# Seven products for the down-projection of a SwiGLU block, with its results added to the residual in DRAM

## The reference

```
x = x + gate2 * SwiGLU(RMSNorm(x) * (1 + scale2) + shift2)
swiglu(h) = (silu(h @ w_gate) * (h @ w_up)) @ w_down      # D_FF = 2816 = 22 tiles of 128
```

## Time and profile before

| | us |
|---|---|
| median of three runs | 940.18 |
| the profiled execution | 943.49 |
| its span, first to last instruction | 941.6 |
| TensorE (PE) busy | 919.5 (98%) |
| VectorE busy | 596.2 (63%) |
| ScalarE busy | 405.5 (43%) |
| mean busy share of the DMA engines in the seven-product stages | 0.72 to 0.75 |

### The profile page before, as it was taken

How to read it: one execution, slowest core, us unless ns; L and a number is a source line. 1 busy time by engine, 2 the same in 40 slices (tenths; PEclk the granted TensorE clock), 3 DMA queues, 4 the chain that set the end, 5 groups by cost and what they waited for, 6 DMA issues and landing times.

```text
span 941.6 us, 15995 instructions
## 1 busy us (share of the span) xinstructions
PE 919.5 (98%) x6385; PEld 861.3 (91%) x6385; DVE 596.2 (63%) x1115; ACT 405.5 (43%) x809; POOL 80.5 (9%) x103
## 2 busy tenths in 40 slices
PE   5999999999999999999999999999999999999998
PEld 5689888778887899999999999999999999999998
DVE  3557898899688752332447966743577763367752
ACT  4564344666767722222246644421344431244430
POOL 0000000000000000000000122101233200133100
PEclk7799999999999999999999999999999999999999
DMA  9854343442444123422203278543687843377631
GB/s 370 321 180 157 134 149 120 154 144 68 136 146 152 63 68 90 180 68 90 68 23 109 72 179 166 158 124 79 154 169 177 184 145 112 79 168 188 169 111 70
DMA packets 45546, 129.35 MB, mean 137 GB/s; under 512 B 5216, under 2 KB 10464, under 8 KB 44320
## 3 DMA queue, kind: packets, MB, share of 16 engines
q1 hardware_dynamic: 32288, 102.64, 32.4%
q0 software_dynamic: 12464, 24.91, 14.8%
q10 hardware_dynamic: 720, 0.77, 0.2%
HBM read 114.02 MB, written 4.33 MB: 126 GB/s over the span
## 4 chain that ended last, share of the span: by engine, by line
PE 80%; DMA 7%; DVE 7%; issue 2%; ACT 2%; SPq 1%; DVEq 0%; POOLq 0%; ACTq 0%
PE ps L1589 38%; PE ps L1946 15%; PE ps L1685 13%; DMA stage<-stage 5%; PE ps L1893 4%; PE ps L1811 3%; PE ps L1785 2%; PE ps L1796 2%; PE ps L1638 1%; DVE w_lo L1462 1%; PE ps L1709 1%; DMA x<-w_ada 1%; DVE scr L1499 1%; DVE scr L1107 1%; DMA vec<-vecs 1%
## 5 line engine op out<-in xcount | busy, mean ns | idle before, releaser
L1070 DVE TENSOR_TENSOR w_lo<-stage,w_hi 128x1024 fp32r<-128x1024 f32 x56 | 68.3, 1222 | 77.4 <-ACT w_hi L640 77.2
L1589 PE MATMUL ps<-y_hi,w_hi 128*128 128x320 f32 x480 | 109.6, 309 | 1.6 <-DVE w_lo L1506 1.6
L1589 PE MATMUL ps<-y_hi,w_lo 128*128 128x320 f32 x480 | 109.4, 309 | 0.0
L1589 PE MATMUL ps<-y_lo,w_hi 128*128 128x320 f32 x480 | 109.3, 309 | 0.0
L985 ACT ACTIVATE w_hi<-stage 128x512 fp32r<-128x512 f32 x114 | 67.9, 624 | 89.3 <-DMA stage<-stage 47.7
L640 ACT ACTIVATE w_hi<-stage 128x1024 fp32r<-128x1024 f32 x56 | 59.1, 1061 | 91.4 <-PE ps L1589 50.9
L1462 DVE TENSOR_TENSOR w_lo<-stage,w_hi 128x512 fp32r<-128x512 f32 x114 | 76.3, 685 | 30.6 <-ACT w_hi L985 30.6
L1946 PE MATMUL ps<-m_hi,w_hi 128*128 128x320 f32 x304 | 93.9, 309 | 0.0
L1946 PE MATMUL ps<-m_lo,w_hi 128*128 128x320 f32 x304 | 93.9, 309 | 0.0
L1946 PE MATMUL ps<-m_hi,w_lo 128*128 128x320 f32 x304 | 93.9, 309 | 0.0
L1589 PEld LDWEIGHTS ps<-y_hi,w_hi 128*128 128x128 f32 x480 | 80.2, 188 | 2.1 <-DVE w_lo L1506 2.1
(11 more groups left out here) (210 smaller groups left out, 1995.4 us busy)
## 6 DMA issues: line engine op xcount, KB each, us to landing
stage<-w_main SPq DMA_DIRECT2D x118, 512.0 KB, 3.7
x<-w_ada SPq DMA_DIRECT2D x23, 512.0 KB, 4.6
scr<-w_main POOLq DMA_DIRECT2D x38, 256.0 KB, 4.6
stage<-stage POOLq DMA_DIRECT2D x38, 256.0 KB, 3.3
qk<-w_ada SPq DMA_DIRECT2D x7, 1024.0 KB, 11.7
stage<-w_main POOLq DMA_DIRECT2D x19, 256.0 KB, 5.0
bb<-rpb SPq DMA_DIRECT2D x16, 256.0 KB, 4.2
qk<-w_ada SPq DMA_DIRECT2D x5, 512.0 KB, 3.7
```

What stands on the lines that cost most here:

```text
L1070: dve.tensor_tensor(w_lo[:, slot, :], stage[:, slot, :], w_hi[:, slot, :].bitcast(F32), ALU.subtract).then_inc(lo_done, 1)
L1589: ins = pe.matmul(out[:, half, :], wt[:, w_slot, w], rt[:, rk, half * TH:(half + 1) * TH], start=start and n == 0, stop=stop and n == 2)
```

## The change

- The down-projection is done by seven products too: two output tiles by two halves of the part's hidden tiles by two halves of the tokens. All work from the fourth hidden tile on is one list of 31 jobs (`JOBS`): 5 gate/up jobs and 4 down jobs, 8 and 4, 6 and 4. A down job has 7 x 4 x 3 matmuls in the first two parts and 7 x 3 x 3 in the last (`job_half`: blocks of 384 columns in place of 512). For every job POOL makes the sums of weights.
- The blocks of the hidden tiles (T1 to T4 of activations) are made per part on DVE and split (`y_sums`, `y_sums_high`, `y_sums_low`).
- The residual isn't held in SBUF any more. POOL copies `x` to `y_t` in one transfer (2.6 MB) when it is complete, and each down result, multiplied by gate2 on ACT (`scaled`), is added to `y_t` by a POOL transfer of 320 KB with accumulate: 24 in all (`add_result`). The eight writes of `x` by SP and the 24 `add_gated` on DVE go away.
- The products come in the order A11, S1, A12, S4, S2, S3, A22 (A11, A12, S2, S1, S3, S4, A22 before), so the gate tile's first half and second half are complete after the third and the fifth product. A22 has two places among the split weights.

The order of POOL's instructions and of ACT's and DVE's loops is new:

```diff
-            for g in range(sum(FF_PARTS) - N_STD):
...
+            pool.wait_ge(x1_done, 8)
+            pool.dma_start(y_t.rearrange("p k t -> p (k t)"), x[:, :]).then_inc(x_out, 16)
+            def add_result(j, second):
+                d, n = down_number(j), JOBS[j][2] + second
+                i = d % 2 * 2 + second
+                pool.wait_ge(r_done, 2 * d + second + 1)
...
+                pool.dma_start(y_t[:, n, :], kept[i], accum_op=ALU.add).then_inc(r_out[i], 16)
...
+            for j in range(len(JOBS)):
+                more = j + 1 < len(JOBS)
+                if j and JOBS[j - 1][1] is None:
+                    add_result(j - 1, 1)
+                if more:
+                    s1_s3_first(j + 1)
+                    s2_s3(j + 1)
+                    s4(j + 1)
+                if JOBS[j][1] is None:
+                    add_result(j, 0)
+            add_result(len(JOBS) - 1, 1)
```

`JOBS[j][1]` is the hidden tile of a gate/up job and None for a down job. On ACT:

```diff
+            def scaled(j, second):
...
+                act.wait_ge(c21_done if second else c12_done, j + 1)
...
+                for kind, t in ((0, slice(0, CTX)), (1, slice(CTX, T))):
+                    ins = act.activation(kept[i][:, t], (low_sb if second else high_sb)[:, t], ACT.Identity,
+                                         scale=mod[:, g + kind:g + kind + 1])
+                ins.then_inc(r_done, 1)
...
+            for j in range(len(JOBS)):
+                f, more = JOBS[j][1], j + 1 < len(JOBS)
+                ended = JOBS[j - 1][1] if j else N_STD - 1
+                if ended is not None:
+                    y_high(ended)
+                else:
+                    scaled(j - 1, 1)
+                if more:
+                    left_high("A11", j + 1)
+                copy_p1(j)
+                if ended is not None:
+                    y_sums_high(ended)
+                if more:
+                    left_high("S1", j + 1)
+                    left_high("A22", j + 1)
+                    left_high("A12", j + 1)
+                if f is not None:
+                    half_tanh(j, 0)
+                if more:
+                    left_high("S2", j + 1)
+                if f is not None:
+                    half_tanh(j, 1)
+                else:
+                    scaled(j, 0)
+                if more:
+                    left_high("S4", j + 1)
+                    left_high("S3", j + 1)
+            scaled(len(JOBS) - 1, 1)
```

On DVE and PE:

```diff
+            for j in range(len(JOBS)):
...
+                if j:
+                    c21(j - 1)
+                if ended is not None:
+                    times_up(j - 1) if j else gated_up(ended)
+                left_low("S4", j)
+                left_low("S3", j)
+                if ended is not None:
+                    y_low(ended)
+                    y_sums(ended)
+                if more:
+                    left_low("A11", j + 1)
+                if ended is not None:
+                    y_sums_low(ended)
+                c11(j)
+                if more:
+                    left_low("S1", j + 1)
+                    left_low("A22", j + 1)
+                    left_low("A12", j + 1)
+                u2_v_c12(j)
+                if more:
+                    left_low("S2", j + 1)
+                c22_u3(j)
+                if f is not None:
+                    gate_times(j)
...
+            for j in range(len(JOBS)):
...
+                    free = dict(A11=(p1_copied, j), S1=(v_done, j), A12=(c11_done, j), S4=(c12_done, j),
+                                S2=(v_done, j), S3=(c22_done, j), A22=(c21_done, j))
+                for op in LEFT:
+                    pe.wait_ge(*free[op])
+                    product(op, j)
```

More of the change, by code:

```diff
@@ L590, in _ @@
                 load_unit(u, u % RING)
[L591 to L593 removed]
             sp.wait_ge(out_kv, 64)
[L595 removed]
+            sp.wait_ge(x_out, 16)
+            for i in range(4):
+                sp.wait_ge(r_out[i], 16 * 2 * len(FF_PARTS))
         @block.gpsimd
@@ L981, in left_high @@
                 else:
[L982 to L990, removed]
+                    act.wait_ge({"S1": s1_sum, "S2": s2_sum, "S3": s3_sum, "S4": s4_sum}[op], 16 * (j + 1))
@@ new lines, in left_high, with copy_p1 @@
+                act.wait_ge(*slot_free(op, j))
+                slot, at = left_place(op, j)
+                act.activation(w_hi[:, slot, at:at + job_half(j) * P], left_stage(op, j), ACT.Copy).then_inc(left_hi[op], 1)
+            def copy_p1(j):
+                act.wait_ge(left_used["A11"], j + 1)
+                if j and JOBS[j - 1][1] is not None:
+                    act.wait_ge(a32_done, JOBS[j - 1][1] + 1)
+                elif j:
+                    act.wait_ge(r_done, 2 * down_number(j))
@@ L1018, in _ @@
             t_high(1)
-            a_high(0)
+            y_high(0)
             gate_tanh(1)
@@ L1497, in products_gated, with gate_times, times_up @@
+            def gate_times(j):
+                dve.wait_ge(tanh_done, JOBS[j][1] + 1)
+                own.mark(dve.scalar_tensor_tensor(out=ft_sb, in0=ft_sb, scalar=1.0, in1=high_sb, op0=ALU.add, op1=ALU.mult))
+            def times_up(j):
+                part, f, _ = JOBS[j]
+                i, half = tile_of(f)
                 own.wait()
-                dve.wait_ge(c12_done, g + 1)
-                dve.scalar_tensor_tensor(out=fp[f % 2], in0=up_sb, scalar=0.5, in1=ft[f % 2],
+                dve.wait_ge(c21_done, j + 1)
+                if part and i < half:
+                    dve.wait_ge(r_out[i], 16 * 2 * part)
+                dve.scalar_tensor_tensor(out=product_of(f), in0=low_sb, scalar=0.5, in1=ft_sb,
@@ L1514, in _ @@
             t_sums(1)
-            a_low(0)
+            y_low(0)
             t_low(0)
             t_low(1)
+            y_sums(0)
             gated(1)
@@ L1523, in _ @@
             t_low(3)
-            a_low(1)
+            y_sums_low(0)
+            y_low(1)
+            y_sums(1)
             left_low("S1", 0)
@@ new lines, in right_made, with product @@
+            def right_made(op, j, k):
+                first, half = FF_FIRST[JOBS[j][0]], job_half(j)
+                f = first + k + (half if op in ("A12", "S4") else 0)
+                if op in ("A11", "A12", "S4"):
+                    return a_ready, f + 1
+                return {"S1": y1_lo, "S2": y23_lo_done, "S3": y23_lo_done, "A22": y4_lo}[op], pair_of(f) + 1
+            def product(op, j):
+                pe.wait_ge(left_lo[op], j + 1)
+                if j == 0 and op not in ("A11", "A12", "S4"):
+                    pe.wait_ge(t_ready, ("S1", "S2", "S3", "A22").index(op) + 1)
+                slot, at = left_place(op, j)
+                half = job_half(j)
+                for k in range(half):
+                    if JOBS[j][1] is None and JOBS[j - 1][1] is not None:
+                        pe.wait_ge(*right_made(op, j, k))
```

446 lines of the change are left out of this document (205 added, 241 removed).

## The result

The changed kernel takes 1012.29 us (median of four runs, 1010.64 to 1017.25) against 940.2: ratio 1.077, 95% interval 1.073 to 1.081. It is 72 us slower; 21 were forecast. The profiled execution took 1017.25 us.

What follows compares the result with a forecast made beforehand. The prediction took the kernel before as bound by its number of matmuls on PE, with transfer circles deciding afterwards. Matmuls and idle -21.0, circles +39.4, end +2.2 made +20.6 us on 940.2, so 961 us; 8-in-10 range 944 to 990.

Steps and rivals of the forecast that it cites:

- Matmuls: Down-projection on PE: 924 matmuls in place of 1056, 132 fewer at 0.147 us, -19.4 us; -21.0 with idle time.
- The circle in a down job: Add ahead of S1 on POOL's queue, S1 landing 5.0 plus 0.4: rounds 16.3 us against PE's 12.3; +39.4 us together.
- T: The time at which S4 of job j has landed; the forecast counts its rounds from there.
- The circle in a gate/up job: S4 landing to next S4 landing: 12.5 us, 11.2 in a part's first half; S2 3.3, S4 3.5; nothing lost.
- the thin cover of DVE: Gate/up jobs of second halves: DVE about 12 us against PE's 12.3; taken as 0, up to 5 us at the upper end.
- The lead: End of a part's gate/up jobs: S4 lands 2.2 us ahead of its latest time, 1.5 in the last part's step.
- `scaled` behind T: Down jobs, ACT: `scaled(j-1, 1)` stands behind splits of S4 and S3; otherwise a round would miss by some 0.3 us.
- The end: Last matmul to end of span: C21, `scaled`, POOL and an accumulate's landing, 6.0 us for 3.8, +2.2.
- long transfers: Rival: adds hold the queue twice as long, 1.8 us more in ten rounds, 979; longest landings 988; chance 0.17.
- clock: Rival: PE's clock falls in the waits, four products behind a wait at half pace, 991 us; chance 0.09.
- short landings: Rival: S1 lands after 3.6 + 0.4 and S4 after 3.2, 1.7 less in ten rounds, 944 us; chance 0.13.
- the adds cost nothing: Rival: down rounds stay under 12.3 us, so only the matmuls count, 921.4 us, faster; chance 0.11.

Runs made afterwards that it cites:

- the version with small adds: Against the changed kernel: S1 issued early with adds behind, S3 split before S4, adds cut to 8 of 640 columns (output incomplete); ratio 0.998 to the kernel before.
- the version with plain writes: Against the changed kernel: S1 issued early with adds behind, S3 split before S4, the 24 adds without accumulation (output incomplete); ratio 1.009 to the kernel before.
- The small adds: Against the changed kernel, its queue order kept: every add to `y_t` moves 8 of its 640 columns (output incomplete); ratio 1.044 to the kernel before.
- the better one: Against the changed kernel: S1 of job j+2 issued right behind S4 of job j+1, adds behind it, S3 split before S4; ratio 1.032 with whole adds.
- the filler: Against the changed kernel: 20 small matmuls into an unused bank in each of ten jobs, ahead of products S1 and S4; ratio 1.076 to the kernel before.
- joined adds: Against the changed kernel: S1 early, S3 split first, one 640 KB add per job, last part's units loaded without padding; ratio 1.023 to the kernel before.

## Why the prediction was wrong

The direction, the down jobs as the place and the path of the circle were right. The landing times of the transfers were wrong, in both kinds of job, and they have one thing in common: they were taken from rows in which other transfers stood around them. The measured loss is over three times the forecast. From the issue of S4 of job 1 (552.89) to that of job 30 (996.41) 443.5 us pass. The matmuls of the 29 jobs between need 26 x 12.3 + 3 x 9.2 = 347.4. So 96 us are lost there, where 39.4 were forecast.

- **Matmuls: right.** PE's busy time in the version with small adds is 899.2 us at a clock of 0.995, the "900 us or a little less" of the forecast.
- **The circle in a down job: right in its path, its largest term mis-sized.** Ten rounds took 182.6 us, where 8 x 16.3 + 2 x 14.8 = 160.0 were forecast: 22.6 us of the excess. From T to the issue of S1 it is 3.0 us where 3.3 were forecast, from S2 to S4 3.9 for 3.7. The step that failed is "I take the median 5.0 ... the very place that the add takes, plus 0.4". S1 landed after 7.1 to 9.4 us in the eight rounds of the first two parts and after 6.1 and 5.7 in the last part, 7.4 in the mean of the ten: 2.1 more a round, 21 of the 22.6 us. The place on the queue was the same, the neighbours weren't: an accumulate to DRAM costs more than its bytes (no add landed under 4.5 us, where in the version with plain writes the shortest took 2.4), and the copy for S3, once held back by a wait, follows 0.55 us behind. The small adds confirm the first: with them, S1 lands after 4.8 us in the mean and the round is 15.8. What the copy behind S1 adds wasn't tried by itself.
- **The circle in a gate/up job: wrong.** "Here nothing is lost" failed by its terms "S2's transfer 3.3" and "S4's transfer 3.5". The forecast left out that the split which frees the copy's place now stands behind T, so that the copy and the completion of S3 are issued close ahead of S2 and S4. S4 landed after 4.6 us in the mean, 1.1 more, and from the issue of S2 to that of S4 it took 0.8 more; the steps on ACT and DVE came as forecast (4.75 for 4.7). That is 1.9 us over the forecast's 11.9, of which 0.4 was spare under PE's 12.3. Eighteen rounds (jobs 1 to 6, 10 to 18, 22 to 27) took 248.6 us instead of 18 x 12.3 = 221.4, 27.2 us of the excess. Splitting S3 first took S4's landing back to 3.5 and the rounds to 12.8, and the ratio from 1.077 to 1.061. What is left over 12.3 is S2, which landed after 4.4 us in the mean in that version too; the thin cover of DVE, which the forecast named, isn't what shows.
- **The lead** of 2.2 us in each of the first two parts and 1.5 in the last, which I let the down rounds use up, didn't exist with such gate/up rounds; its 5.9 us are most of the 7 that remain. The forecast also had nothing for the waits for `y_low` at the first down job of each part, 9.1 us in three waits. `y_low` stands on DVE behind the splits of S4 and S3, so it waits for T as well; the chain at the first of them goes on through the splits and the copy for S3, not through PE, so these waits lie beside the circle.
- **`scaled` behind T** was named as the cause. It is on the chain, but moving it ahead gave 0.012 only. "If `scaled(j-1, 1)` were not behind T, a round counted from PE's end would miss by some 0.3 us only" was wrong: the round stayed 5.4 us over 12.3, with S1 landing after 8.6. The weightier choice was the add ahead of S1 (0.032).
- **The end: too small.** From the end of the last product, 1007.6, to 1015.4 it is 7.8 us; 6.0 were forecast, 3.8 were measured before. The last add landed after 5.3 us, where 4.0 were forecast.
- **Rival "long transfers"** was borne out in what it says, that the adds hold up what stands behind them, but its price of 1.8 us a round was too small. Adds of 8 columns give back 2.7 a round in the changed kernel's order, 2.9 in the better one. That an accumulate costs more than a plain write is measured; that it does so because it "reads and writes DRAM" is not.
- **Rival "clock"**: the clock did fall in the waits, as the Trainium skill, "TensorE: Matmul & The Clock Gate", section "Why this matters for your kernels", says it does when PE stands idle between bursts. The trace agrees: after PE's wait of 3.63 us, which ends at 615.7, matmuls follow one another every 0.27 us in place of 0.147, and the granted clock is 0.87 in 615.3 to 702.6. Over the span behind 546 us it was 0.93, which the forecast had named as a sign of being wrong. But when the filler raised the clock, the time didn't follow.
- **Rivals "short landings" and "the adds cost nothing"**: S1 landed after 5.7 us or more in every down round, where the first of them had 4.0. The second would follow by the fit of the Trainium skill, "DMA: Bandwidth & Descriptors", section "Anatomy of one DMA — SWDGE (gpsimd) path", from which 2.6 us for 256 KB is an estimate. S1's landings of 4.0 to 9.4 us disagree by far.

What stays open: why joined adds help more than their load explains; how the load of the unit loads and of the copy divides among the late landings of S1; and why S2 lands late in gate/up rounds. In those that make S2 4 us behind T it took 4.9 to 5.7 us even in the version with S3 split first, where the copy stands 3.8 us ahead of it.

## What to carry to other kernels

A queue that only prepares work can still hold up everything. It does so when an instruction that depends on the end of a round stands ahead of one that starts the next: go through the issuing engine's list and write down every wait ahead of the transfer in question. A wait that the list shows need not cost anything, though. Look whether the next transfer was issued later than its own input allowed, before you call the wait the cause; here the profile's chain goes through a wait that held nothing back by itself.

The landing time of a transfer holds for its neighbours. When a change alters what is issued around it, don't take the median of the old rows: take the longest and add the neighbours' load. An edit that only delays an unrelated copy changes the neighbours too. Before work is moved to transfers, add up what the DMA engines have to do in a round: here they were at 0.73 before the adds came.

## What the runs showed of the hardware

A transfer with accumulate from SBUF to DRAM was dear here. For 24 transfers of 320 KB in otherwise the same kernel, accumulating cost 0.023 of the time beyond a plain write of the same bytes, about 21 us or 0.9 us each, and the shortest landing was 4.4 us against 2.4. An accumulate of 256 KB from SBUF to SBUF took 4.6 us in the mean of eighteen with another transfer issued 1.0 to 2.4 us ahead of it by the same engine, and 3.4 where that one stood 2.8 to 5.5 us ahead. A lower clock of TensorE need not cost anything: raised from 0.962 to 0.985 by filler matmuls in the waits, it left the time where it was, in a kernel whose rounds the transfers set.
